# A hybrid layer step on one core: the projection stage issued in another order

## The reference

```
h = rmsnorm(x, g_mix)                                   # 280 rows of 1024
qkv_a, z_a, b_a, a_a, q_f, k_f, v_f, f_f, gates = split(h @ w_in)
qkv = silu(causal_conv(concat(state_conv, qkv_a), conv_w))   # delta-rule branch: q, k, v of 4 heads of 128
beta, g, lf = sigmoid(b_a), -exp(a_log) * softplus(a_a + dt_bias), log_sigmoid(f_f + b_forget)
qf, kf = rmsnorm per head (8 heads of 64)               # forgetting attention
sample rows: scores of qf against cache_k[page_table] (8 pages of 128 rows each), then softmax, values
x = x + (sigmoid(gate_a) * (o_a @ p_a) + sigmoid(gate_f) * (o_f @ p_f)) @ w_o
y = x + moe(rmsnorm(x, g_ffn))                          # 32 experts, top 4
```

## Time and profile before

| | us |
|---|---|
| median of 3 runs | 1609.44 (1607.33 to 1609.75) |
| device time of the profiled execution | 1607.82 |
| its span, first to last instruction | 1606.2 |
| mean granted clock of TensorE | 0.919 |
| TensorE busy | 1430.5 (89%) |
| VectorE, ScalarE, GpSimd busy | 546.5, 166.4, 155.7 |

### The profile page before, as it was taken

The page is one execution under the profiler, slowest core; times in us unless marked ns, Lnnn a source line. Parts: engine busy times, 40 slices in busy tenths (PEclk is TensorE's granted clock), DMA queues, the critical chain, the costliest instruction groups (busy, mean ns, idle before and its releaser), DMA issues.

```text
span 1606.2 us, 17392 instructions
## 1 busy us (share of the span) xinstructions
PE 1430.5 (89%) x6568; PEld 661.2 (41%) x6568; DVE 546.5 (34%) x1102; ACT 166.4 (10%) x366; POOL 155.7 (10%) x133
## 2 busy tenths in 40 slices
PE   5999696989987992999999999899899899899897
PEld 4657475965542632333333233233233233233232
DVE  2138746732233222323233232232232232232233
ACT  1133212112101010000000000000000000000000
POOL 1024454400012000000000000000000000000000
PEclk7999797975568995799999999999999999999999
DMA  8535472100047818469999999999999999999997
GB/s 236 175 120 190 139 264 105 31 23 1 0 158 226 349 52 333 195 254 428 427 429 430 428 428 429 428 429 429 428 430 426 430 429 427 429 429 429 428 429 295
DMA packets 72777, 487.61 MB, mean 304 GB/s; under 512 B 11039, under 2 KB 15647, under 8 KB 48158
## 3 DMA queue, kind: packets, MB, share of 16 engines
q1 hardware_dynamic: 57430, 449.81, 68.3%
q10 hardware_dynamic: 10032, 20.02, 3.5%
q0 software_dynamic: 5280, 17.31, 3.1%
HBM read 481.24 MB, written 5.97 MB: 303 GB/s over the span
## 4 chain that ended last, share of the span: by engine, by line
DMA 41%; PE 20%; DVE 1%; issue 0%; SPq 0%; ACT 0%; DVEq 0%; ACTq 0%
DMA wu<-in_w_up 39%; PE bank L1658 16%; DMA bdn<-in_b_down 1%; PE bank L1668 1%; PE bank L1682 1%; PE bank L1649 1%; PE bank L1709 0%; PE bank L1692 0%; DVE u L1813 0%; DVE u L1810 0%; PE bank L1640 0%; DVE xr L1767 0%; SPq L1333 0%; ACT ysb L1737 0%; DVEq L1572 0%
## 5 line engine op out<-in xcount | busy, mean ns | idle before, releaser
L1658 PE MATMUL bank<-wu,xT 128*64 128x512 f32 x992 | 225.0, 598 | 47.1 <-DMA wu<-in_w_up 47.1
L1658 PE MATMUL bank<-wd,hT 128*64 128x512 f32 x1024 | 226.8, 595 | 0.0
L1658 PE MATMUL bank<-wg,xT 128*64 128x512 f32 x992 | 220.8, 598 | 0.0
L478 PE MATMUL bank<-hT,wg 128*128 128x280 f32 x640 | 160.3, 411 | 0.1
L1658 PEld LDWEIGHTS bank<-wu,xT 128*64 128x64 f32 x992 | 66.3, 136 | 203.7 <-issue 115.5
L1767 DVE TENSOR_TENSOR xr<-xr,bank 128x512 f32<-128x512 f32 (+1 forms) x204 | 130.2, 679 | 51.2 <-PE bank L1682 29.3
L478 PEld LDWEIGHTS bank<-hT,wg 128*128 128x128 f32 x640 | 124.6, 196 | 34.2 <-issue 3.5
L1658 PEld LDWEIGHTS bank<-wd,hT 128*64 128x64 f32 x1024 | 70.7, 137 | 153.9 <-issue 121.1
L1658 PEld LDWEIGHTS bank<-wg,xT 128*64 128x64 f32 x992 | 67.6, 137 | 150.1 <-issue 135.9
L1615 POOL DMA_INDIRECT xg<-h_dram,idx x33 | 31.6, 959 | 921.7 <-DVE idx L1756 921.7
L1668 PE MATMUL bank<-ysb,comb 64*128 64x512 f32 (+1 forms) x396 | 116.7, 632 | 0.8 <-ACT ysb L1737 0.8
(11 more groups left out here) (413 smaller groups left out, 1344.9 us busy)
## 6 DMA issues: line engine op xcount, KB each, us to landing
wd<-in_w_down SPq DMA_DIRECT2D x64, 2048.0 KB, 25.7
wu<-in_w_up SPq DMA_DIRECT2D x62, 2048.0 KB, 26.2
wg<-in_w_gate SPq DMA_DIRECT2D x62, 2048.0 KB, 24.6
wg<-in_w_in ACTq DMA_DIRECT2D x9, 2048.0 KB, 9.5
wd<-in_cache_k SPq DMA_DIRECT2D x64, 256.0 KB, 3.4
wd<-in_cache_v SPq DMA_DIRECT2D x32, 256.0 KB, 4.6
wd<-in_cache_v POOLq DMA_DIRECT2D x32, 256.0 KB, 3.9
wg<-in_w_in SPq DMA_DIRECT2D x2, 2048.0 KB, 10.4
```

The source lines that it names most:

```text
L478: last = mm(ps(b, P, T), w[:, k, P * c:P * c + P], hT[:, k], start=k == 0, stop=k == 7)
L1658: last = mm(bank[b][64 * a:64 * a + 64, :], x[:, k % 4, 64 * (k // 4):64 * (k // 4) + 64], W[buf][:, k, 512 * a:512 * a + 512], start=name ...
```

## The change

- The order of the "a" banks: query sums, `qD`, the eight broadcasts, key sums, and the rest.
- SP: behind the first weights come the page table and the norm gains, then the second weights, and only then the small weights, biases and convolution rows. The load of `state_delta` and the copy of `state_conv` go behind the whole loop of key pages.
- TensorE: no small projections and convolution columns ahead of the queries; query sums behind k1; `qD` behind k3; all eight broadcasts between v0 and v1; small projections and convolution columns behind v2.
- ScalarE: the copies in the same order; the exponentials and logarithms of the small columns behind the stores of the values.
- VectorE: key sums 0 and 1 behind the squares of the keys, then the small columns, the norms of the keys, key sums 2 to 6; then each convolution part with three key sums behind it (7 to 9, 10 to 12, 13 to 15).

```diff
-        "a": [f"nq{n}" for n in range(4)] + [f"nk{n}" for n in range(4)] + ["qD", "kD", "cvp0", "cvs0"]
-             + [f"qB{n}" for n in range(NS)] + ["cvp1", "cvs1"] + [f"krow{n}" for n in range(3)] + ["cvp2", "cvs2"]
+        "a": [f"nq{n}" for n in range(4)] + ["qD"] + [f"qB{n}" for n in range(NS)] + [f"nk{n}" for n in range(4)]
+             + ["kD", "cvp0", "cvs0", "cvp1", "cvs1"] + [f"krow{n}" for n in range(3)] + ["cvp2", "cvs2"]
...
-            proj_cols([f"k{c}" for c in range(4)])
-            pe.wait_ge(S["bd64_set"], 2)
-            pe.wait_ge(S["sq_done"], 1)
-            for c in range(4):
-                sums(f"nq{c}", bd64[:, :], sq[:, c])
+            def query_sums(tile):
+
+                if tile == 2:
+                    pe.wait_ge(S["bd64_set"], 2)
+                    pe.wait_ge(S["sq_done"], 1)
+                    for c in range(4):
+                        sums(f"nq{c}", bd64[:, :], sq[:, c])
...
+            proj_cols([f"k{c}" for c in range(4)], query_sums)
+            pe.wait_ge(S["normed"], 4)
+            rows_of("qD", lambda c, c0, n: qk[:, c, c0:c0 + n], NP, NS)
             w = chunk_in()
             for t in range(2):
+                if t == 1:
+                    evac_wait(pe, "a", "qD")
+                    for b in range(NS):
+                        fill_wait(pe, "a", f"qB{b}")
+                        done("a", mm(ps(bank_of("a", f"qB{b}"), P, 512), ident[0:NS, b:b + 1].to_broadcast([NS, P]), qD[:, :],
+                                     start=True, stop=True))
...
+            small()
+            conv_columns()
...
             evac_wait(dve, "proj", "k3")
             squares(qk[:, 4:8])
+            for n in range(2):
+                key_sums(n)
+            small_columns()
             for c in range(4):
                 normalize(qk[:, 4 + c], f"nk{c}", gq[:, 1:2], 4 + c)
+            for n in range(2, 7):
+                key_sums(n)
...
-                for n in range((0, 0, 3)[part], (0, 3, 6)[part]):
+                for n in range(7 + 3 * part, 10 + 3 * part):
                     key_sums(n)
...
-            for n in range(6, 2 * NS):
-                key_sums(n)
```

More of the change, by code:

```diff
@@ L235, in _ @@
             weights(0)
+            sp.dma_start(pts[:, :], i["page_table"].rearrange("(o b) n -> o (b n)", o=1)).then_inc(S["pts_in"], 16)
+            for half in range(2):
+                sp.dma_start(gq[64 * half:64 * half + 64, 0:1], i["qn_g"].rearrange("a d -> d a")).then_inc(S["gq_in"], 16)
+                sp.dma_start(gq[64 * half:64 * half + 64, 1:2], i["kn_g"].rearrange("a d -> d a")).then_inc(S["gq_in"], 16)
+            weights(1)
             sp.dma_start(wsm[:, :, 0:8], w_in[:, :, C_BA:C_BA + 8]).then_inc(S["wsm_in"], 16)
@@ L366, in _ @@
             weights(2)
+            for c in range(2):
+                proj(f"k{c}", copy(qk[:, 4 + c], P, T))
             for c in range(4):
+                norm(f"nq{c}", 1.0 / HD, c)
+            for c in range(2, 4):
                 proj(f"k{c}", copy(qk[:, 4 + c], P, T))
             weights(3)
-            for c in range(4):
-                norm(f"nq{c}", 1.0 / HD, c)
+            misc("qD", copy(qD[:, :], NS, 512))
             proj("v0", copy(vr[:, 0], P, 512))
+            for b in range(NS):
+                misc(f"qB{b}", copy(qB[:, b], P, 512))
             proj("v1", copy(vr[:, 1], P, 512))
@@ L449, in _, with small, conv_columns @@
             pe.wait_ge(S["hT_done"], 5)
[L450 to L461, removed]
+            def small():
+                pe.wait_ge(S["wsm_in"], 32)
+                b = bank_of("v", "small")
+                for t, (_, _, c0, n) in enumerate(ROWS):
+                    for k in range(KT):
+                        last = mm(bank[b][0:n, 16 * t:16 * t + 16], hT[:, k, c0:c0 + n], wsm[:, k], start=k == 0, stop=k == 7)
+                done("v", last)
+            def conv_columns():
+                pe.wait_ge(S["cr_in"], 32)
+                b = bank_of("v", "cw")
+                for c in range(12):
+                    last = nc.tensor.transpose(bank[b][:, 28 * c:28 * c + 28], cr[:, P * c:P * c + P], ident[0:28, 0:28])
+                done("v", last)
             chunk = [0]
@@ L485, in _, with rows_of @@
             proj_cols([f"q{c}" for c in range(4)])
-            proj_cols([f"k{c}" for c in range(4)])
-            pe.wait_ge(S["bd64_set"], 2)
-            pe.wait_ge(S["sq_done"], 1)
-            for c in range(4):
-                sums(f"nq{c}", bd64[:, :], sq[:, c])
+            def query_sums(tile):
[4 more added lines that the diff above has]
+                        sums(f"nq{c}", bd64[:, :], sq[:, c])
+            def rows_of(name, src, c0, n):
+                fill_wait(pe, "a", name)
+                b = bank_of("a", name)
+                for c in range(4):
+                    last = nc.tensor.transpose(bank[b][0:n, P * c:P * c + P], src(c, c0, n), ident[:, :])
+                done("a", last)
+            proj_cols([f"k{c}" for c in range(4)], query_sums)
+            pe.wait_ge(S["normed"], 4)
+            rows_of("qD", lambda c, c0, n: qk[:, c, c0:c0 + n], NP, NS)
             w = chunk_in()
             for t in range(2):
+                if t == 1:
+                    evac_wait(pe, "a", "qD")
+                    for b in range(NS):
+                        fill_wait(pe, "a", f"qB{b}")
+                        done("a", mm(ps(bank_of("a", f"qB{b}"), P, 512), ident[0:NS, b:b + 1].to_broadcast([NS, P]), qD[:, :],
+                                     start=True, stop=True))
                 fill_wait(pe, "proj", f"v{t}")
@@ L579, in _ @@
             tt(hT[:, :, 272:280], src[:, :, 32:40], spread(gmix[:, :], 2, NS), ALU.mult).then_inc(S["hT_done"], 1)
[L582 to L603, removed]
             def squares(src):
@@ L621, in _ @@
             squares(qk[:, 4:8])
-            for c in range(4):
-                normalize(qk[:, 4 + c], f"nk{c}", gq[:, 1:2], 4 + c)
             def key_sums(n):
@@ L630, in key_sums, with small_columns @@
                                         ).then_inc(S[f"kslot{n % 4}_used"], 1)
+            def small_columns():
+                full_wait(dve, "v", "small")
+                dve.wait_ge(S["bias_in"], 32)
+                dve.wait_ge(S["smz_zeroed"], 1)
+                b = bank_of("v", "small")
+                for t, (_, _, _, n) in enumerate(ROWS):
+                    ins = tt(smz[0:n, t], bank[b][0:n, 16 * t:16 * t + 16], bias16[0:n, :], ALU.add)
+                ins.then_inc(S["v_evac"], 1)
+                evac_wait(dve, "v", "small")
+                stt(sml[:, :, :], smz[:, :, :], -1.0, smz[:, :, :], ALU.mult, ALU.min).then_inc(S["sm_abs"], 1)
+                full_wait(dve, "v", "cw")
+                src = ps(bank_of("v", "cw"), P, 12, 28)
+                nc.vector.tensor_copy(cwt[:, :, :], src)
+                for c in range(12):
+                    ins = nc.vector.tensor_copy(xs[:, c, :, 0:3], src[:, c, 4:28].rearrange("p (b w) -> p b w", w=3))
+                ins.then_inc(S["v_evac"], 1)
+                dve.wait_ge(S["sm_ln"], 1)
+                dve.wait_ge(S["ea_done"], 1)
+                stt(sm[:, :, 0:4], smz[:, :, 0:4], 0.0, sml[:, :, 0:4], ALU.min, ALU.subtract)
+                stt(sm[:, :, 8:16], smz[:, :, 8:16], 0.0, sml[:, :, 8:16], ALU.min, ALU.subtract)
+                me.link(stt(sm[:, :, 4:8], smz[:, :, 4:8], 0.0, sml[:, :, 4:8], ALU.max, ALU.add))
+                stt(sm[:, :, 4:8], sm[:, :, 4:8], -1.0, spread(ea[:, :], 1, 4), ALU.mult, ALU.mult).then_inc(S["sm_logs"], 1)
+            for n in range(2):
+                key_sums(n)
+            small_columns()
+            for c in range(4):
+                normalize(qk[:, 4 + c], f"nk{c}", gq[:, 1:2], 4 + c)
+            for n in range(2, 7):
+                key_sums(n)
             dve.wait_ge(S["consts"], 5)
```

36 lines of the change are left out of this document (11 added, 25 removed).

## The result

The changed kernel took 1609.71 us (median of 20 runs, 1604.48 to 1615.93), the kernel before 1606.73 (20 runs beside them, 1601.58 to 1610.40). The ratio is 1.0027, with a 95% interval of 1.0015 to 1.0039: slower by 4.3 us, between 2.4 and 6.3 (the two medians lie 3.0 apart). The profiled execution has a span of 1611.5 us, 5.3 above that of before, and the projection stage alone accounts for 5.0 of them: its last gate product ends at 208.34 + 49.51 = 257.85, and ended at 252.84 before.

What follows compares the result with a forecast made beforehand. VectorE's order, as GpSimd's key products block it, was taken to decide the projection stage's end: squares at 189.5 plus 67.7 gave 257.3, +4.4 us, so 1613.8 us on the median of 1609.44; range 1605.5 to 1621.

Steps and rivals of the forecast that it cites:

- Projection and early products: TensorE's projection starts at 14.1 instead of 30.75; six GpSimd key products run from 59.5 to 87.6, blocking nothing.
- The clock: TensorE's eight 8-row broadcasts in a row: 9 us at half clock level, 4.5 us lost, about 2.5 reaching the end.
- the wait for the sixth key product: VectorE's key sums, before the first convolution part: a slot's refill wait expected to cover the rest of the clock loss.
- Part 0: First convolution part on VectorE meets key products 7 to 10 and takes 22.5 us, bounds 7.1 and 24.
- Part 1: Second convolution part on VectorE: key product 11 from 147 holds one instruction; 7.0 + 4.1 us, to 155.0.
- Sums 11 and 12, part 2: VectorE's key sums 10 to 12 end at 162.9; third convolution part, blocked by key products, ends at 180.8, squares at 189.5.
- From the squares to the end: Rest of the projection stage takes 67.7 instead of 75.7 us: norms unblocked, the 5.68 wait gone; TensorE idles 27 before it.
- Even: Rival, chance 0.25: clock stays up, key refills wait for the whole weights load; stage ends at 252.9, time 1609.5.
- Fair shares: Rival, chance 0.2: key and weight loads served side by side, products fall into the second convolution part; about +4 more, 1618.
- The faster side: Rival, chance 0.07 in full, 0.1 for a small piece: each convolution part takes 7.1; stage ends at 228, time 1584.5.

Runs made afterwards that it cites:

- the six executions: Profiled executions sharing the changed kernel's TensorE order: itself, short products, late sums, sums in old places, later gate-weights load, one blocked part; stretch to A0 39.6 to 44.0 us.
- the two grouped runs on the changed order: Changed kernel with its eight query broadcasts split into two groups of four, or into four pairs; ratios to before 1.0031 and 1.0038.
- the run with the later load: Changed kernel with the first gate weights' load issued behind the last Silu instead of behind tile A11; ratio to before 1.0082.
- another order of the sums: Changed kernel with key sums 2 to 5 behind the first convolution part and 6 to 15 last, or only 7 to 15 last; 1580.45 and 1578.12 us.

## Why the prediction was right

It forecast +4.4 us, from a stage end of 257.3; the stage ended at 257.85, and the ratio says +4.3. That they agree so closely is in part luck: the squares came 2.1 later than forecast, and what follows them was 1.4 shorter. The time itself, 1613.8, lies 4.1 above the measured median: 2.7 of that because it was put on the median of three runs of before (1609.44), which over 20 runs is 1606.73, the rest because the medians lie only 3.0 apart. By its steps:

- **Projection and early products.** Projection from 13.60 (forecast 14.1), six products from 57.94 to 84.83 (59.5 to 87.6): right. They block nothing, as said.
- **The clock.** 4.5 us were to be lost at the lower level. Against rows at the higher level v1 lost 1.7 (8.73 - 7.04), the broadcasts 1.3 (9.15 - 8 x 0.98), the convolution columns 0.5 and the key sums behind them 1.1: 4.6. The size was right, the place only in part: a third of it fell behind the small products, and A0 behind them lost another 1.8 (5.70 - 3.94) that the forecast did not have. Key norms were done at 97.4 (98).
- **Luck in the clock's term.** The row that the term was taken from shows TensorE busy for only 1.32 of 2.00 us, so idle time could have made that fall; and of the six executions the profiled one spent the least on the stretch. That 2.5 of the 4.5 would reach the end fits the two grouped runs on the changed order: there A0 started 5.4 and 3.0 later than in the changed kernel, and the end came 3.0 and 1.7 later. But it was not the wait for the sixth key product that took up the rest, since that stayed at 5.5 to 5.7; most of it went into the waits of sums 11 and 12, together 5.1 and 5.3 instead of 6.9.
- **Part 0.** Four products, 24.1 us, where 22.5 was taken from bounds of 7.1 to 24. Less ran ahead of GpSimd here, 1.3 us instead of 3.1: the four TENSOR_SCALAR were through, and the first product starts 0.09 behind the first SCALAR_TENSOR_TENSOR.
- **Part 1.** The one step that failed in its place. Product 11 was to run at 147 and hold one instruction (11.1 us); the gate weights' load, issued at 143.6, put off this product as well, to 151.30, and the part ran free (7.1). That the load collides, and that the part gets by more cheaply for it, was right. The load's landing in the changed kernel:

```profile
L360 ACTq DMA_DIRECT2D wg<-in_w_in x1: 547/547/547, 143.6 to 143.6; - x1
...
DMA to landing us min/median/max: 15.3/15.3/15.3
```

- **Sums 11 and 12, part 2.** What part 1 gained, the sums gave back in waits of 1.91 and 5.02: part 2 starts at 165.5 (162.9) and takes 17.6 (17.9). Squares 191.56 (189.5).
- **From the squares to the end.** 66.3 us (67.7): the norms ran free and the wait of 5.68 went, as said. The early z and the late squares make a wait of 31.38 (27).

Even named 1609.5, by chance nearer to the measured 1609.71 than the forecast's 1613.8, since both were put on the high median of before; but it stood for no change, which the ratio excludes, and its conditions did not occur: the clock fell, and a key page issued behind the weights, at 144.8, landed at 151.2, long before them (143.6 + 15.3 = 158.9). Fair shares was half right: the load took 15.3 instead of 9.7, while the five key pages issued from 144.8 to 149.9 beside it took 6.4 to 8.7 to land; in the run with the later load the pages of the same two refills took 2.4 to 3.9. So both were slowed. The Trainium skill, "DMA: Bandwidth & Descriptors", section "Queues, rings and completion order", has each DMA engine go round its queues packet by packet, and these numbers agree. But the price had the wrong sign: it is without the collision that products fall into part 1. The faster side's figure, 228 us when no part holds up the squares, was met within half a us by another order of the sums (227.60 and 228.00); the changed order itself gave nothing of it, since its sums free slots just ahead of each part.

## What to carry to other kernels

When two engines hold each other up, an earlier start on a third is worth only what the order of the held one lets through: here the same early start came with a gain of some 5 us over before with the key sums in their old places, with a loss of 4 with the places that the change gave them, and with a gain of 24 to 27 when few of them stood ahead of the squares. Look at what each instruction releases, not only at what it waits for: a sum that frees a slot just ahead of a chain of short instructions makes each of these wait for a long one. And where a long instruction must fall on some chain, let it all fall on the one with slack, then stop releasing more.

## What was not expected of the hardware

TensorE's clock fell to its lower level in stretches without an idle gap: over the broadcasts of 8 rows when eight or four stood in a row, and, where they stood in pairs, over or at the end of the products of 16 columns (7.58 us at the lower level for what takes 4.64 at the higher). The stretch from v0 to A0 differed by 4.4 us between executions of the same order. And a TENSOR_SCALAR of one tensor input is held by a product as well: four of them took 11.67 us instead of 1.17. The trace of before had it already (four in the third part took 6.86).
